# A 31-tap convolution between three engines: the low halves of 32 weight chunks made by accumulating DMAs, and twelve taps of each odd block moved from TensorE to VectorE

## The chip, the cores and the metric

The kernel runs on one core of one Trainium2 chip. The metric is the device time of one execution in microseconds (us). Before the change it is 2404.21 us, the median of 3 runs (2402.06 to 2404.46).

## The reference

Two layers over a residual stream of 256 tokens by 2048 channels, in float32. What matters here is the first layer's conformer group:

```
u = rms_norm(h) @ w_in                      # 2048 -> 4096, split into a_val, a_gate, xr, gr (1024 each)
ya = a_val * sigmoid(a_gate)                # GLU, 1024 channels
ya = causal_depthwise_conv(ya, conv_a_w, conv_a_b)     # 31 taps for each channel
ya = silu(layer_norm(ya, ln_a_g, ln_a_b))
yb = rg_lru(causal_depthwise_conv(xr, 4 taps)) * gelu(gr)
h  = h + concatenate([ya, yb]) @ w_out
```

After it come a squared-ReLU MLP (2048 -> 8192 -> 2048), a per-layer embedding with a sigmoid gate, and a second layer with stick-breaking attention and the same MLP and gate.

## The kernel before, in words

**Layout.** Activations are held transposed: a tile is 128 channels by 256 tokens. The weights stream from HBM in 812 chunks of 512 KB (128 partitions x 4 row tiles x 256 columns), numbered in one fixed order: `C_GLU` = 34 begins the GLU part of the input projection (32 chunks), `C_OUTB` = 66 the half of the output projection that takes the RG-LRU channels (16 chunks), `C_PLE0` = 82 the embedding projection.

**Splitting.** A product in float32 is made of three float32r products: hi x hi, hi x lo and lo x hi. So each chunk is split: ScalarE copies `raw` into the hi half of a slot of `spl`, rounding it (`split` of ScalarE, `copy` at L636), VectorE writes `raw - hi` into the lo half (`split` of VectorE, L1037), and TensorE uses both (`chunk`, L398 for the 512-column matmuls, L404 for the 256-column ones; 16 matmuls a chunk). `raw` has 4 buffers (`NRAW`) and `spl` has 8 slots (`NSPL`). The sync engine loads chunk m once the lo of chunk m - 4 is made (`lo_ready`); ScalarE writes slot m % 8 once TensorE has used chunk m - 8 (`chunk_used`). ScalarE and VectorE split chunk m + 8 in the place of their programs that belongs to chunk m.

**Groups.** 256 output channels are one group: 4 chunks in the GLU part, 2 in the output halves. A group has two PSUM banks in turn with the next one. At its end ScalarE copies the 256 columns of the cross products (`take_cross`), VectorE adds them to the rest (`take_sum`, L1073), and a group may only start when the sum of the group two before it is taken.

**The convolution.** The 8 blocks of 128 GLU channels are convolved in pairs. Pair c - 1 is convolved while the groups of pair c go through TensorE (`glu_pair(c)`, c = 1, 2, 3), and the last pair beside the first four groups of `C_OUTB`. The even block of a pair is wholly VectorE's (`conv`, L1363 to L1369): 31 taps that alternate between two partial sums. The odd block is shared: TensorE does `CA_PE` = 25 taps as products with diagonal matrices `dg` (L576), which ScalarE builds out of the identity (`tap_matrices`, L892), and VectorE does `CA_VE` = 6 (L1375, L1378). `conv_end` (L1388) adds the two. TensorE's taps stand in three portions in a pair: behind the first group (`taps(0)`), in the middle of the second (`taps(1)`) and behind it (`taps(2)`); in `C_OUTB` one quarter stands behind each of four groups.

**Order.** Every engine has its program written out, in order, with semaphores. In `glu_pair` VectorE does, for q = 0 to 7, four steps of `conv`, one tap of the odd block (q < 6), and one `split`; after q = 3 it takes the value group (`glu_value`), at the end the gate group (`glu_gate`), which waits for a sigmoid of ScalarE (L869). In the first pair two RG-LRU operations are added (L1399 and a `lo_of`). ScalarE does an eighth of the matrices and one split for each q, `take_cross` after q = 3 and 7, and then waits for VectorE before the sigmoid. After the four `C_OUTB` groups the LayerNorm follows: two reductions on VectorE, two small matmuls in the middle of groups 5 and 7, and a chain up to the embedding projection (L461). GpSimd issues no DMA and is idle after its first microseconds.

Of the kernel before, what the change touches and what calls it, by code (L numbers as in the profile page):

```python
# [30 lines left out]
T = 256  # L31
DA = D // 2
# [35 lines left out]

H_OUTB, H_OUTA, H_MLP0, H_GATE0, H_OUT1, H_MLP1, H_GATE1 = 0, 8, 16, 48, 56, 64, 96
NDG = 14  # L70
CA_PE = 25
CA_VE = CA - CA_PE
CSTEPS = CA + 1 + CA_VE
LAM_STEPS = 17


GAIN = 0
# [12 lines left out]
def trunk(nc, xT, pT, par, w_in, w_rg_a, w_rg_x, w_out, w_qkv, w_o, w_up, w_down, w_proj, w_gate, outT):  # L90
    with ExitStack() as ctx:
# [3 lines left out]
        def sem(name):  # L95
            return ctx.enter_context(nc.semaphore(name))
# [58 lines left out]
        raw_landed = [sem(f"raw_landed{i}") for i in range(NRAW)]  # L155
        hi_ready = sem("hi_ready")
        lo_ready = sem("lo_ready")
        chunk_used = sem("chunk_used")
        par_landed = sem("par_landed")
        x_landed = [sem(f"x_landed{i}") for i in range(4)]  # L160
# [69 lines left out]
        def counts(base, turns):  # L230


            return base > 0 or not isinstance(turns, int)

        def bcast(ap, n):
            return ap.unsqueeze(1).broadcast_to([P, n, ap.shape[-1]])

# [11 lines left out]
        def _(sp):  # L249
            def load(m, it, src):  # L250

                if counts(m - NRAW + 1, it):
                    sp.wait_ge(lo_ready, it * 8 + (m - NRAW + 1))
                sp.dma_start(raw[:, m % NRAW, :, :], src).then_inc(raw_landed[m % NRAW], 16)

            def load_group(m, it, w, col, row0=0, rows=(0, 4, 8, 12)):
                for j, r in enumerate(rows):
                    src = w[bass.ds(row0 + r * P, 4 * P), bass.ds(col, 256)]
                    load(m + j, it, src.rearrange("(t p) n -> p t n", p=P))
# [39 lines left out]

            def half_square(m, w, row0):  # L300

                with sp.Fori(0, 2) as i:
                    for s in range(4):
                        load_group(m + 2 * s, i, w, i * 1024 + 256 * s, row0, (0, 4))

            def load_x(k):
                sp.dma_start(h[:, 4 * k:4 * k + 4, :], xT[4 * k * P:(4 * k + 4) * P, :].rearrange(
# [22 lines left out]
            with sp.Fori(1, 4) as i:  # L330
                load_group(C_REC, i, w_in[0], i * 256 + 2 * DA)
                load_group(C_REC + 4, i, w_in[0], i * 256 + 2 * DA + DB)
            with sp.Fori(0, 4) as i:
                load_group(C_GLU, i, w_in[0], i * 256)
                load_group(C_GLU + 4, i, w_in[0], i * 256 + DA)
            half_square(C_OUTB, w_out[0], DA)
            load_ple(C_PLE0, 0)
            half_square(C_OUTA, w_out[0], 0)
# [42 lines left out]
                               pattern=[[1, P]], channel_multiplier=-1).then_inc(consts_ready, 1)  # L381


        @block.tensor
        def _(pe):
            def chunk(b, m, it, x, kt0, first, last, tokens_out=False, releases=1):

                pe.wait_ge(lo_ready, it * 8 + (m + 1))
                w = spl[:, m % NSPL, :, :, :]
                for q in range(4):  # L390
                    kt, start, stop = kt0 + q, first and q == 0, last and q == 3
                    for o in range(2):
                        c = slice(o * P, (o + 1) * P)
                        if tokens_out:

                            pe.matmul(ps[:, b + o, :], x[:, kt, 0, c], w[:, q, :, :], start=start, stop=False)  # L396
                        else:
                            pe.matmul(ps[:, b + o, :], w[:, q, 0, c], x[:, kt, :, :], start=start, stop=False)  # L398
                    for o in range(2):
                        c = slice(o * P, (o + 1) * P)  # L400
                        if tokens_out:
                            mm = pe.matmul(ps[:, b + o, 0:256], x[:, kt, 1, c], w[:, q, 0, :], start=False, stop=stop)  # L402
                        else:
                            mm = pe.matmul(ps[:, b + o, 0:256], w[:, q, 1, c], x[:, kt, 0, :], start=False, stop=stop)  # L404
                mm.then_inc(chunk_used, releases)
# [44 lines left out]
            def ple(g, m, layer, units):  # L450

                for u in units:
                    c, b = m + 1 + u // 2, 2 * (u % 2)
                    pe.wait_ge(sum_ready, g + u - 1)
                    pe.wait_ge(lo_ready, c + 1)
                    for k in range(2):
                        x = spl[:, m % NSPL, 2 * layer + k, :, :]
                        for o in range(2):

                            w = spl[:, c % NSPL, 2 * k + u % 2, :, o * P:(o + 1) * P]  # L460
                            pe.matmul(ps[:, b + o, :], w[:, 0, :], x, start=(k == 0), stop=False)  # L461
                            mm = pe.matmul(ps[:, b + o, 0:256], w[:, 1, :], x[:, 0, :], start=False, stop=(k == 1))
                    if u < 7:
                        mm.then_inc(ple_done, 1)
                    else:
                        mm.then_inc(chunk_used, 5)
# [113 lines left out]
            gemm(G_GLU, 0, C_GLU, 0, XA)  # L580
            pe.wait_ge(rg_act, 4)
            gemm(G_GLU + 1, 0, C_GLU + 4, 0, XA)
            with pe.Fori(1, 4) as c:
                for s in range(2):
                    def taps(part):
                        conv(c - 1, c * CA_PE - CA_PE, part, 3)

                    gemm(G_GLU + s, c * 2, C_GLU + 4 * s, c, XA, mid=None if s == 0 else lambda: taps(1))
                    taps(2 * s)


# [42 lines left out]
        def _(act):  # L634
            def copy(out, in_, scale=1.0):
                return act.activation(out, in_, ACT.Copy, scale=scale)  # L636

            def split(m, it=0):

                if m < CHUNKS:  # L640
                    act.wait_ge(raw_landed[m % NRAW], it * (16 * 8 // NRAW) + 16 * (m // NRAW + 1))
                    if counts(m - NSPL + 1, it):
                        act.wait_ge(chunk_used, it * 8 + (m - NSPL + 1))
                    copy(spl[:, m % NSPL, :, 0, :], raw[:, m % NRAW, :, :]).then_inc(hi_ready, 1)

            def period(m, it, k=4):
                for q in range(k):
# [247 lines left out]
            def glu_pair(c):  # L895
                for q in range(8):
                    tap_matrices(c - 1, c * CA_PE - CA_PE, q, 8)
                    split(C_GLU + NSPL + q, c)
                    if isinstance(c, int) and q == 4:

                        act.wait_ge(rg_vec, 6)
                        copy(XB[:, 8:16, 0, :], pp[:, 0:8, :]).then_inc(rg_act, 1)
                    if q % 4 == 3:
                        take_cross(G_GLU + q // 4, c * 2, group_done(C_GLU + q - 3, c))
                glu_gate(c)

            act.wait_ge(rg_vec, 5)
            glu_pair(1)
            with act.Fori(2, 4) as c:
                glu_pair(c)  # L910

            def ple_cross(g, m, layer, units):
# [118 lines left out]
        def _(dve):  # L1031
            def split(m, it=0):

                if m < CHUNKS:
                    dve.wait_ge(hi_ready, it * 8 + (m + 1))
                    s = spl[:, m % NSPL, :, :, :]
                    dve.tensor_tensor(s[:, :, 1, :], raw[:, m % NRAW, :, :], s[:, :, 0, :].bitcast(F32),  # L1037
                                      ALU.subtract).then_inc(lo_ready, 1)
# [304 lines left out]
            def conv(pair, base, q):  # L1343
# [3 lines left out]

                first, y2t, second = y[:, bass.ds(pair * 2, 1), :], y2[:, :].unsqueeze(1), y[:, bass.ds(pair * 2 + 1, 1), :]

                def step(n):  # L1350
                    return n + min(n // 4, CA_VE)

                if q == 0:
                    dve.wait_ge(glu_ready, pair + 1)
                for n in range(4 * q, 4 * q + 4):
# [12 lines left out]
                    else:  # L1368
                        r = dve.tensor_tensor(first, first, y2t, ALU.add)  # L1369
                    r.then_inc(conv_step, 1)  # L1370
                if q < CA_VE:
                    k = CA_PE + q
                    x, w = glu[:, bass.ds(pair * 2 + 1, 1), k:k + T], par_col(pair * (2 * CA) + (CONV_A_W + CA + k))
                    if q == 0:
                        r = dve.tensor_scalar(second, x, w, par_col(pair * 2 + (1 + CONV_A_B)), ALU.mult, ALU.add)  # L1375
                    else:
                        dve.wait_ge(conv_step, base + 5 * q)
                        r = dve.scalar_tensor_tensor(out=second, in0=x, scalar=w, in1=second, op0=ALU.mult, op1=ALU.add)  # L1378
                    r.then_inc(conv_step, 1)
                if q == 7:  # L1380
                    dve.wait_ge(conv_step, base + CSTEPS)

# [7 lines left out]
            def glu_pair(c):  # L1390
                for q in range(8):
                    conv(c - 1, c * CSTEPS - CSTEPS, q)
                    split(C_GLU + NSPL + q, c)
                    if q == 3:
                        glu_value(c)
                    if isinstance(c, int) and q == 2:

                        dve.wait_ge(rg_vec, 5)
                        dve.tensor_tensor(pp[:, 0:8, :], r_, pp[:, 8:16, :], ALU.mult).then_inc(rg_vec, 1)  # L1399
                    if isinstance(c, int) and q == 6:  # L1400
                        dve.wait_ge(rg_act, 8)
                        lo_of(XB, 8, 8, pp[:, 0:8, :]).then_inc(yb_tiles, 1)
                glu_gate(c, lambda: conv_end(c - 1))

            glu_pair(1)
            with dve.Fori(2, 4) as c:
                glu_pair(c)

            def ple_sums(g, units):
# [183 lines left out]
```

## Time and profile before

| what | value |
|---|---|
| median of 3 runs | 2404.21 us |
| profiled execution, its own time | 2405.38 us |
| its span | 2403.7 us |
| TensorE clock granted, mean | 0.992 |
| TensorE busy | 2353.1 us (98%) |
| VectorE busy | 1600.6 us (67%) |
| ScalarE busy | 1277.2 us (53%) |
| GpSimd busy | 2.1 us |

Shares are over the whole span; a stage has its own. A busy share of TensorE says that matmuls are in flight, not that they run at their peak. Idle time of an engine counts only if another waits for it. The convolution stands between about 155 and 279 us of the span.

### The profile page before, as it was taken

The numbers are of one execution on the slowest core, as the hardware profiler recorded it, in microseconds if no ns is written. First come the engines' busy times: TensorE is split into PE (matmuls) and PEld (weight loads), VectorE is DVE, ScalarE is ACT, GpSimd is POOL, SyncE is SP. The second block draws the span as 40 slices with busy tenths as digits, with TensorE's granted clock in tenths as the row PEclk, the third lists the DMA queues.
The fourth block names the chain that finished last, engine by engine and source line by source line (L and its number), as shares of the span: only waits on it lengthen the run. The fifth ranks groups of instructions, "written<-read, shape, count | busy, mean of one in ns | idle before, by whom it ended". The sixth has DMA issues, their size and how long they took to land.

```text
span 2403.7 us, 39317 instructions
## 1 busy us (share of the span) xinstructions
PE 2353.1 (98%) x13454; PEld 2052.8 (85%) x13454; DVE 1600.6 (67%) x1892; ACT 1277.2 (53%) x1632; POOL 2.1 (0%) x15
## 2 busy tenths in 40 slices
PE   7999999999999999999999999999999999999997
PEld 6878878888888888888888888888888888888886
DVE  7789987655555555667766666766556556556665
ACT  6665565444444545555565666555445445445553
POOL 0000000000000000000000000000000000000000
PEclk9999999999999999999999999999999999999998
DMA  7644456655665666555655554656656566565553
GB/s 232 210 123 135 130 163 193 193 185 182 197 187 181 195 189 185 187 189 166 201 172 177 168 157 142 208 183 189 193 180 198 185 187 192 188 188 187 190 161 105
DMA packets 432146, 431.03 MB, mean 179 GB/s; under 512 B 13136, under 2 KB 430032, under 8 KB 432080
## 3 DMA queue, kind: packets, MB, share of 16 engines
q1 hardware_dynamic: 432080, 430.20, 57.5%
q8 instruction: 36, 0.59, 0.1%
q14 instruction: 30, 0.25, 0.0%
HBM read 428.05 MB, written 2.10 MB: 179 GB/s over the span
## 4 chain that ended last, share of the span: by engine, by line
PE 91%; DVE 4%; ACT 2%; issue 1%; DMA 1%; DVEq 0%; SPq 0%; ACTq 0%
PE ps L398 56%; PE ps L404 28%; PE ps L396 2%; PE O L576 2%; DVE spl L1037 1%; PE ps L402 1%; ACT spl L636 1%; PE ps L461 0%; PE O L505 0%; DVE tv L1073 0%; PE Z L479 0%; DMA raw<-in_w_o 0%; DMA raw<-in_w_in 0%; DVE nacc L1101 0%; DVE tv L1099 0%
## 5 line engine op out<-in xcount | busy, mean ns | idle before, releaser
L1037 DVE TENSOR_TENSOR spl<-raw,spl 128x1024 fp32r<-128x1024 f32 x810 | 979.6, 1223 | 521.1 <-ACT spl L636 482.5
L636 ACT ACTIVATE spl<-raw 128x1024 fp32r<-128x1024 f32 x810 | 842.9, 1055 | 685.6 <-PE ps L404 640.9
L398 PE MATMUL ps<-XA,spl 128*128 128x512 f32 x3072 | 971.1, 398 | 15.9 <-DVE spl L1037 10.9
L398 PE MATMUL ps<-XB,spl 128*128 128x512 f32 x3072 | 967.5, 396 | 0.5 <-DVE pp L1073 0.5
L404 PEld LDWEIGHTS ps<-XA,spl 128*128 128x128 f32 x3072 | 579.2, 189 | 137.2
L404 PEld LDWEIGHTS ps<-XB,spl 128*128 128x128 f32 x3072 | 577.1, 188 | 136.4
L404 PE MATMUL ps<-XA,spl 128*128 128x256 f32 x3072 | 605.2, 278 | 0.0
L404 PE MATMUL ps<-XB,spl 128*128 128x256 f32 x3072 | 603.6, 278 | 0.0
L398 PEld LDWEIGHTS ps<-XA,spl 128*128 128x128 f32 x3072 | 470.4, 189 | 17.6 <-issue 11.5
L398 PEld LDWEIGHTS ps<-XB,spl 128*128 128x128 f32 x3072 | 468.3, 189 | 1.6 <-issue 0.8
L1073 DVE TENSOR_TENSOR tv<-cross,ps 128x512 f32<-128x512 f32 x208 | 141.6, 681 | 39.4 <-ACT cross L636 39.2
L636 ACT ACTIVATE cross<-ps 128x512 f32<-128x512 f32 x224 | 130.3, 582 | 68.8 <-PE ps L404 57.2
L716 ACT ACTIVATE tv<-tv 128x512 f32<-128x512 f32 x64 | 40.4, 631 | 138.5 <-DVE tv L1130 138.5
L1117 DVE TENSOR_TENSOR h<-h,tv 128x512 f32 (+1 forms) x104 | 72.0, 692 | 21.1 <-DVE tv L1073 18.8
L396 PE MATMUL ps<-spl,XB 128*128 128x512 f32 x256 | 80.7, 397 | 0.0
L689 ACT ACTIVATE tv<-h 128x512 f32 (+1 forms) x56 | 35.4, 632 | 59.0 <-DVE h L1117 56.1
L1066 DVE TENSOR_TENSOR XB<-tv,XB 128x512 f32 (+1 forms) x32 | 22.2, 692 | 54.0 <-ACT XB L636 54.0
L402 PEld LDWEIGHTS ps<-spl,XB 128*128 128x128 f32 x256 | 48.1, 188 | 11.4
L1066 DVE TENSOR_TENSOR XA<-tv,XA 128x512 f32 (+1 forms) x32 | 22.2, 692 | 53.4 <-ACT XA L636 53.4
L576 PE MATMUL O<-glu,dg 128*128 (+1 forms) x200 | 47.1, 389 | 3.7 <-ACT dg L892 3.7
L402 PE MATMUL ps<-spl,XB 128*128 128x256 f32 x256 | 50.4, 278 | 0.0
L1367 DVE SCALAR_TENSOR_TENSOR y<-glu,params,y 128x256 f32<-128x256 f32 (+1 forms) x116 | 48.7, 478 | 0.8 <-DVE glu L1079 0.5
(145 smaller groups left out, 885.7 us busy)
## 6 DMA issues: line engine op xcount, KB each, us to landing
raw<-in_w_up SPq DMA_DIRECT2D x256, 512.0 KB, 3.9
raw<-in_w_down SPq DMA_DIRECT2D x256, 512.0 KB, 3.5
raw<-in_w_qkv SPq DMA_DIRECT2D x96, 512.0 KB, 4.4
raw<-in_w_in SPq DMA_DIRECT2D x64, 512.0 KB, 4.2
raw<-in_w_gate SPq DMA_DIRECT2D x64, 512.0 KB, 4.3
raw<-in_w_out SPq DMA_DIRECT2D x32, 512.0 KB, 3.4
raw<-in_w_o SPq DMA_DIRECT2D x32, 512.0 KB, 4.6
raw<-in_w_proj SPq DMA_DIRECT2D x8, 512.0 KB, 4.3
```

Source lines behind the costliest of these rows:

```text
L396: pe.matmul(ps[:, b + o, :], x[:, kt, 0, c], w[:, q, :, :], start=start, stop=False)
L398: pe.matmul(ps[:, b + o, :], w[:, q, 0, c], x[:, kt, :, :], start=start, stop=False)
L402: mm = pe.matmul(ps[:, b + o, 0:256], x[:, kt, 1, c], w[:, q, 0, :], start=False, stop=stop)
L404: mm = pe.matmul(ps[:, b + o, 0:256], w[:, q, 1, c], x[:, kt, 0, :], start=False, stop=stop)
L576: pe.matmul(O[:, 0, 0:256], dg[:, k % NDG, :], glu[:, bass.ds(pair * 2 + 1, 1), k:k + T], start=(k == 0), stop=(k == CA_PE - 1), skip_grou ...
L636: return act.activation(out, in_, ACT.Copy, scale=scale)
L716: act.activation(tv[:, :, :], tv[:, :, :], ACT.Square).then_inc(up_sq, 1)
L1037: dve.tensor_tensor(s[:, :, 1, :], raw[:, m % NRAW, :, :], s[:, :, 0, :].bitcast(F32), ALU.subtract).then_inc(lo_ready, 1)
L1066: return dve.tensor_tensor(X[:, bass.ds(t0, n), 1, :], v, X[:, bass.ds(t0, n), 0, :].bitcast(F32), ALU.subtract)
L1073: dve.tensor_tensor(tv[:, :, :] if out is None else out, cross[:, :, :], ps[:, b:b + 2, 0:256], ALU.add).then_inc(sum_ready, 1)
L1117: dve.tensor_tensor(ht, ht, tv[:, :, :], ALU.add).then_inc(res_ready, 1)
L1367: r = dve.scalar_tensor_tensor(out=o, in0=x, scalar=w, in1=o, op0=ALU.mult, op1=ALU.add)
```

## The change

The 32 chunks 50 to 81 (`SUMMED`) get their lo in another way. ScalarE writes hi as before and then also -hi, a second copy with scale -1, into the lo half. GpSimd waits for it and issues an accumulating DMA from `raw` onto the lo half, SBUF to SBUF, so that raw - hi stands there. TensorE and the load that reuses the `raw` buffer wait for that DMA. VectorE has no split for them. `CA_PE` goes from 25 to 13, so VectorE does 18 taps of each odd block, spread evenly over the 32 steps of `conv`. Some loops (`Fori`) of the sync, tensor, scalar and vector programs are written out, as the chunk number must be known.

```
-CA_PE = 25
+CA_PE = 13
+SUMMED = tuple(range(C_GLU + 16, C_PLE0))
+def cuts(m):
+    return m - sum(1 for k in SUMMED if k < m)
+def sums(m):
+    return sum(1 for k in SUMMED if k < m and k % NSPL == m % NSPL)
...
+        def lo_there(engine, m, it):
+            if m in SUMMED:
+                engine.wait_ge(lo_summed[m % NSPL], 16 * sums(m) + 16)
+            elif counts(m + 1, it):
+                engine.wait_ge(lo_ready, it * 8 + cuts(m + 1))
...                                             # sync, load()
-                if counts(m - NRAW + 1, it):
-                    sp.wait_ge(lo_ready, it * 8 + (m - NRAW + 1))
+                lo_there(sp, m - NRAW, it)
...                                             # gpsimd
+            for n, m in enumerate(SUMMED):
+                pool.wait_ge(neg_ready, n + 1)
+                pool.dma_start(spl[:, m % NSPL, :, 1, :].bitcast(F32), raw[:, m % NRAW, :, :],
+                               accum_op=ALU.add).then_inc(lo_summed[m % NSPL], 16)
...                                             # tensor, chunk() and ple()
-                pe.wait_ge(lo_ready, it * 8 + (m + 1))
+                lo_there(pe, m, it)
...                                             # scalar, split()
+                    if m in SUMMED:
+                        copy(spl[:, m % NSPL, :, 1, :], raw[:, m % NRAW, :, :], -1.0).then_inc(neg_ready, 1)
...                                             # vector, split()
-                if m < CHUNKS:
+                if m < CHUNKS and m not in SUMMED:
...                                             # vector, conv()
+                def seconds(n):
+                    return n * CA_VE // (CA + 1)
                 def step(n):
-                    return n + min(n // 4, CA_VE)
+                    return n + seconds(n)
...
-                if q < CA_VE:
-                    k = CA_PE + q
...
+                    if seconds(n + 1) > seconds(n):
+                        j = seconds(n)
+                        x = glu[:, bass.ds(pair * 2 + 1, 1), CA_PE + j:CA_PE + j + T]
...
+                            dve.wait_ge(conv_step, base + n0 + 1 + j)
+                            r = dve.scalar_tensor_tensor(out=second, in0=x, scalar=w, in1=second,
+                                                         op0=ALU.mult, op1=ALU.add)
```

## Rows read from the trace of the kernel before

**Rows 1.** The page: span; busy us, share, instructions by engine.
```profile
span 2403.7 us, 39317 instructions
PE 2353.1 (98%) x13454; PEld 2052.8 (85%) x13454; DVE 1600.6 (67%) x1892; ACT 1277.2 (53%) x1632; POOL 2.1 (0%) x15
```

**Rows 2.** Windows: stretch, length; PE, PEld, DVE, ACT, POOL busy; clock, DMA, GB/s.
```profile
154.90:279.00 124.10, 124.10 (x654) 108.03 (x655) 117.38 (x212) 69.52 (x143) 0.00 (x0) 0.99 0.43 133
301.50:325.00 23.50, 18.60 (x86) 14.95 (x85) 17.52 (x20) 18.54 (x27) 0.00 (x0) 0.85 0.23 69
```

**Rows 3.** The chain of waits in order of time: start, us, what.
```profile
154.87 5.40 PE O L576 x16
189.95 3.46 PE O L576 x16
199.00 3.46 PE O L576 x16
208.05 3.89 PE O L576 x18
241.18 3.89 PE O L576 x18
275.17 3.02 PE O L576 x14
```

**Rows 4.** Who waited for whom from 154.9 to 279 us: total, times, longest.
```profile
ACT spl L636 <- PE ps L404: 32.5, 20, 4.3
ACT tv L869 <- DVE tv L1079: 18.0, 3, 9.5
PE O L576 <- ACT dg L892: 3.7, 1, 3.7
```

**Rows 5.** Timeline of VectorE, second pair: start, us, instruction, tiles, idle before.
```profile
190.84 1.67 DVE L1367 SCALAR_TENSOR_TENSOR y<-glu,params,y  x4
192.42 0.48 DVE L1378 SCALAR_TENSOR_TENSOR y<-glu,params,y  x1
192.82 1.22 DVE L1037 TENSOR_TENSOR spl<-raw,spl 128x1024 fp32r<-128x1024 f32 x1
193.95 1.67 DVE L1367 SCALAR_TENSOR_TENSOR y<-glu,params,y  x4
200.19 0.68 DVE L1073 TENSOR_TENSOR tv<-cross,ps 128x512 f32<-128x512 f32 x1
201.99 1.90 DVE L1367 SCALAR_TENSOR_TENSOR y<-glu,params,y  x4 [0.27 <-DVE glu L1079]
214.17 0.68 DVE L1073 TENSOR_TENSOR tv<-cross,ps 128x512 f32<-128x512 f32 x1
217.91 0.41 DVE L1363 TENSOR_SCALAR y<-glu,params  x1 [0.93 <-DVE glu L1312]
```

**Rows 6.** Groups by line: the RG-LRU product of the first pair, on VectorE.
```profile
L1399 DVE TENSOR_TENSOR pp<-rg,pp 128x2048 f32<-128x2048 f32 x1 | 2.3, 2283 | 0.0
```

**Rows 7.** Tile y, each pair's last step: ns min/median/max, first to last start.
```profile
L1388 DVE TENSOR_TENSOR y<-y,O x4: 410/414/420, 185.9 to 279.1; 128x256 f32<-128x256 f32 x2, 128x256 f32 x2
```

**Rows 8.** Timeline of ScalarE: the start, and two rows of the second pair.
```profile
153.76 0.97 ACT L892 ACTIVATE dg<-ident,params 128x128 f32<-128x128 f32 x3
189.27 1.04 ACT L636 ACTIVATE spl<-raw 128x1024 fp32r<-128x1024 f32 x1
190.22 0.97 ACT L892 ACTIVATE dg<-ident,params 128x128 f32<-128x128 f32 x3
```

**Rows 9.** DMA: page's queue; issues in two stretches; a window of the sync engine.
```profile
q1 hardware_dynamic: 432080, 430.20, 57.5%
raw<-in_w_in SPq DMA_DIRECT2D x12, 512.0 KB, 3.7
h<-in_xT SPq DMA_DIRECT2D x4, 512.0 KB, 8.7
10.00:20.00 10.00, 1.00 1.10 352
```

More of the change, by code:

```diff
@@ L157, in trunk @@
         lo_ready = sem("lo_ready")
+        neg_ready = sem("neg_ready")
+        lo_summed = [sem(f"lo_summed{i}") for i in range(NSPL)]
         chunk_used = sem("chunk_used")
@@ L300, in half_square @@
             def half_square(m, w, row0):
-                with sp.Fori(0, 2) as i:
-                    for s in range(4):
-                        load_group(m + 2 * s, i, w, i * 1024 + 256 * s, row0, (0, 4))
+                for s in range(8):
+                    load_group(m + 2 * s, 0, w, 256 * s, row0, (0, 4))
             def load_x(k):
@@ L332, in _ @@
                 load_group(C_REC + 4, i, w_in[0], i * 256 + 2 * DA + DB)
-            with sp.Fori(0, 4) as i:
-                load_group(C_GLU, i, w_in[0], i * 256)
-                load_group(C_GLU + 4, i, w_in[0], i * 256 + DA)
+            for i in range(4):
+                load_group(C_GLU + 8 * i, 0, w_in[0], i * 256)
+                load_group(C_GLU + 8 * i + 4, 0, w_in[0], i * 256 + DA)
             half_square(C_OUTB, w_out[0], DA)
@@ L454, in ple @@
                     pe.wait_ge(sum_ready, g + u - 1)
-                    pe.wait_ge(lo_ready, c + 1)
+                    lo_there(pe, c, 0)
                     for k in range(2):
@@ L582, in _ @@
             gemm(G_GLU + 1, 0, C_GLU + 4, 0, XA)
-            with pe.Fori(1, 4) as c:
+            for c in range(1, 4):
                 for s in range(2):
@@ L586, in taps @@
                         conv(c - 1, c * CA_PE - CA_PE, part, 3)
-                    gemm(G_GLU + s, c * 2, C_GLU + 4 * s, c, XA, mid=None if s == 0 else lambda: taps(1))
+                    gemm(G_GLU + 2 * c + s, 0, C_GLU + 8 * c + 4 * s, 0, XA, mid=None if s == 0 else lambda: taps(1))
                     taps(2 * s)
@@ L897, in glu_pair @@
                     tap_matrices(c - 1, c * CA_PE - CA_PE, q, 8)
-                    split(C_GLU + NSPL + q, c)
-                    if isinstance(c, int) and q == 4:
+                    split(C_GLU + NSPL + 8 * c + q)
+                    if c == 1 and q == 4:
                         act.wait_ge(rg_vec, 6)
@@ L903, in glu_pair @@
                     if q % 4 == 3:
-                        take_cross(G_GLU + q // 4, c * 2, group_done(C_GLU + q - 3, c))
+                        take_cross(G_GLU + 2 * c + q // 4, 0, group_done(C_GLU + 8 * c + q - 3, 0))
                 glu_gate(c)
@@ L908, in _ @@
             glu_pair(1)
-            with act.Fori(2, 4) as c:
+            for c in range(2, 4):
                 glu_pair(c)
@@ L1370, in conv @@
                     r.then_inc(conv_step, 1)
-                if q < CA_VE:
-                    k = CA_PE + q
[L1373 to L1379, printed above, removed]
+                    if seconds(n + 1) > seconds(n):
+                        j = seconds(n)
+                        x = glu[:, bass.ds(pair * 2 + 1, 1), CA_PE + j:CA_PE + j + T]
+                        w = par_col(pair * (2 * CA) + (CONV_A_W + CA + CA_PE + j))
+                        if j == 0:
+                            r = dve.tensor_scalar(second, x, w, par_col(pair * 2 + (1 + CONV_A_B)), ALU.mult, ALU.add)
+                        else:
+                            n0 = max(k for k in range(n) if seconds(k + 1) > seconds(k))
+                            dve.wait_ge(conv_step, base + n0 + 1 + j)
+                            r = dve.scalar_tensor_tensor(out=second, in0=x, scalar=w, in1=second,
+                                                         op0=ALU.mult, op1=ALU.add)
+                        r.then_inc(conv_step, 1)
                 if q == 7:
@@ L1392, in glu_pair @@
                     conv(c - 1, c * CSTEPS - CSTEPS, q)
-                    split(C_GLU + NSPL + q, c)
+                    split(C_GLU + NSPL + 8 * c + q)
                     if q == 3:
                         glu_value(c)
-                    if isinstance(c, int) and q == 2:
+                    if c == 1 and q == 2:
                         dve.wait_ge(rg_vec, 5)
                         dve.tensor_tensor(pp[:, 0:8, :], r_, pp[:, 8:16, :], ALU.mult).then_inc(rg_vec, 1)
-                    if isinstance(c, int) and q == 6:
+                    if c == 1 and q == 6:
                         dve.wait_ge(rg_act, 8)
@@ L1405, in _ @@
             glu_pair(1)
-            with dve.Fori(2, 4) as c:
+            for c in range(2, 4):
                 glu_pair(c)
```

## The prediction

> **What bounds the kernel now.** I read the page first: TensorE is busy for 98% of the span [rows 1], so only what shortens TensorE's path, or makes it wait, can count. The windows come next. From 154.9 to 279 us, where the convolution runs, TensorE is busy all 124.1 us, VectorE 117.4 and ScalarE 69.5; the DMA engines are at 0.43 and GpSimd does nothing [rows 2]. The chain of waits says what TensorE does there: chunks, and between them portions of taps, which lie on the chain themselves [rows 3]. The waits show that it hardly waits (3.7 us for the first matrices), while ScalarE waits 32.5 us for TensorE's slots and 18.0 us for VectorE's end of a pair [rows 4]. So TensorE bounds this stage, with VectorE close behind, and room is on ScalarE, GpSimd and the DMA engines.
>
> **Unit prices.** On TensorE a tap is two records, so nine take 3.89 us: 0.432 a tap. The portion in the middle of a group ends at 199.00 + 3.46 = 202.46, and the next begins at 208.05, with two chunks between: 5.59 us, 2.79 a chunk [rows 3]. On VectorE four taps and the next start are 192.42 - 190.84 = 1.58 us, 0.395 a tap; a lo difference takes 193.95 - 192.82 = 1.13 of its queue. glu_value takes 201.99 - 200.19 = 1.80 and glu_gate with its waits 217.91 - 214.17 = 3.74 [rows 5]. On ScalarE a rounding copy takes 190.22 - 189.27 = 0.95 and a matrix 0.97 / 3 = 0.32 [rows 8].
>
> **TensorE's taps.** 4 x 12 = 48 taps go, 48 x 0.432 = 20.7 us, all on the path. I walk through it. Portions are now 4, 4 and 5 taps. The first one still waits for ScalarE: from 153.76 [rows 8] it builds a matrix, then copy and negated copy, two matrices, again two copies, and the fourth matrix at 153.8 + 4 x 0.32 + 4 x 0.95 = 158.9 us; the portion ends at about 159.4 instead of 154.87 + 5.40 = 160.3 [rows 3]. Then two chunks, 4 taps, two chunks, 5 taps: 174.5. Four chunks on, the second pair's taps start at 185.7, where they started at 189.95. A pair is then 8 x 2.79 + 13 x 0.432 = 27.9 us, against 33.1 (208.05 to the like portion at 241.18). So the third pair's taps start at 213.6, the output groups at 230.4 (241.18 + 3.89 = 245.1 before), and the last tap ends at 230.4 + 27.9 = 258.3 against 275.17 + 3.02 = 278.2 [rows 3]. If nobody is late, 19.9 us are gained.
>
> **VectorE.** A pair is 49 taps x 0.395 = 19.4, 0.4 for the sum of the two partials, 1.8 and 3.7: 25.3 us; eight differences (9.0 us) left it and twelve taps (4.7) came. The first pair has two more operations of 2.3 us [rows 6] (the second taken as equal): 29.9. It begins about with TensorE's first portion, at 154.7, and the GLU values are ready at 184.6, where TensorE asks at 185.7; then at 209.9, asked at 213.6; the third time at about 235.2, asked at 230.4 + 5.6 = 236.0. The cover is thin, 0.8 us in places. The last pair, 19.8 us and four times 1.4 for the output sums, ends at 261.0, 2.7 us behind TensorE, where its last step began at 279.1 [rows 7] behind 278.2. The chain of the LayerNorm hangs on it and TensorE waits in it later (18.6 of 23.5 us busy [rows 2]). I charge 1.4 us, between 0 (the small matmuls stand further back in groups 5 and 7) and 4 (each tap 0.02 us dearer by its wait).
>
> **ScalarE.** 32 negated copies at 0.95 are 30.4 us more, 48 matrices at 0.32 are 15.4 less. A pair: 16 x 0.95 + 13 x 0.32 + about 2 of crosses and sigmoid (estimated as two copies) = 21 of 27.9 us. Its waits of 32.5 us [rows 4] cover it: nothing. Each cross stands 0.95 later, with a whole group of cover. If the cover were gone it would be at most 12 x 0.95 = 11 us.
>
> **The loops written out** change loads' order in nothing; 0, at most 1 us either way (no row prices a loop's turn).
>
> **The accumulating DMAs.** No row shows one, nor a DMA issued by GpSimd. What they must do follows from the walk. TensorE wants chunk 50's lo at 174.5 and chunk 81's at 258.3 + 7 x 2.79 = 277.8. ScalarE has the first negated copy done at 153.8 + 0.3 + 1.9 = 156.0. Landing: 3.7 us is the nearest load, 8.7 the longest one, those of x behind each other [rows 9]; I take 5, so the first lo is there at 161. Then 31 more may take 277.8 - 161 = 116.8 us, 3.77 us each, before TensorE loses anything. Two limits decide whether that holds.
> - Engine time. A load occupies the 16 engines for 57.5% x 2403.7 / 821 = 1.68 us on average, 524 KB / 352 GB/s = 1.49 when they are full [rows 9]. Beside each load stands now one accumulate of X us. Below it is a plain copy, 1.49. It reads two operands and writes one, three passes where a copy has two: 2.24. With both reads in one line, it is two loads' worth: 2.98 at the full rate, 3.36 at the average. At 2.24 the pace is 3.73, just under 3.77: no stall.
> - Latency. A raw buffer is held for load, two copies and accumulate: (3.7 + 1.9 + 0.3 + L) / 4. L = 5 gives 2.7 us a chunk, 8.7 gives 3.65: no stall. From L = 9.2 it stalls.
> I take X at 2.24, as the queue's 1.49 and 1.68 hold waiting on HBM that a read of SBUF need not have.
>
> The Trainium skill speaks against it in "Collectives: The Full Stack", The bandwidth ceiling: a reduce step has two read descriptors for each chunk on the same read ring, so it runs at about half a copy's rate. That is the second rival's X; no run here shows it so far. Its page "DMA: Bandwidth & Descriptors", Anatomy of one DMA, gives a GpSimd-issued DMA 2.0 us plus bytes / 436 GB/s, by which L would be an estimated 3.2 us and the latency limit harmless.
>
> **Sum.** 2405.4 (the profiled execution) - 19.9 + 1.4 = 2386.9. The profile lies 1.2 us above the median, so 2385.7: I say 2386.
>
> **The rivals.**
> 1. *The DMA engines become the bound, two reads for one.* X = 2.98: pace 4.47, stall 31 x (4.47 - 3.77) = 21.7, net 21.7 - 18.5 = +3.2: 2407. X = 3.36 beside loads of 1.68: pace 5.04, stall 39.4: 2425. TensorE would wait for lo from the third pair on. It decides from X = 2.88, where the pace is 3.77 + 18.5 / 31 = 4.37. For it: 8 chunks of the output part come at 2.79 us with no tap between. Against: a share of only 0.43 now.
> 2. *The slot is held too long.* GpSimd's issuing and the landing take L = 12 us or more, and as all accumulates stand in one queue behind one another, a chunk takes 4.5 us or more: 2407 at 4.5, 2422 at 5, 2453 at 6. From L = 11.6 it is slower than before. For it: GpSimd is a slow issuer for all the rows tell (none), and 8.7 us exists in this trace as a landing. Against: loads land in 3.7 us.
> 3. *Half a stall.* X between 2.3 and 2.9: 2388 to 2404.
> 4. *VectorE is the bound*, each tap at its own 0.48 us [rows 5] instead of 0.395: a pair is 29.5 us, 1.6 above TensorE's, over four pairs some 6 us: 2392. It is part of the forecast's case.
>
> **How the numbers follow.** About 0.2% (4.8 us) is what a measurement of this kernel can tell from no change. Forecast with rival 4: 0.50, all faster, its own range 2381 to 2394. Rival 3: 0.10, of it 0.04 faster, 0.06 within. Rival 1: 0.22, of it 0.08 within and 0.14 slower. Rival 2: 0.18, slower. Faster 0.54, same 0.14, slower 0.32. The range goes from 2381 (no charge for VectorE, taps a little dearer than 0.432) to 2430, which takes in rival 1 and the nearer half of rival 2.
>
> **What would show it.** Right: TensorE still busy throughout from 155 to 258, 104 tap records, the last tap at about 258, VectorE without a difference there, a pair of 27.9 us, ScalarE waiting for slots. The accumulate's landing, the DMA share of the stretch (0.43 now; over 0.9 for rival 1, below it with a long landing for rival 2) and TensorE's waits for a DMA onto the lo half tell the rivals apart. The forecast is wrong if such waits exceed 3 us in total, or if ScalarE's waits turn from TensorE's slots to loads.

## The result, and the profile after

The changed kernel takes 2417.18 us (median of 6 runs, 2411.0 to 2419.44) against 2403.62 of before (6 runs, 2402.06 to 2405.34): ratio 1.0053, 95% interval 1.0042 to 1.0063. It is slower by 13.6 us; 18 us faster was forecast.

The page of the changed kernel, its first rows:

```profile
span 2417.7 us, 38500 instructions
PE 2343.0 (97%) x13358; PEld 2038.5 (84%) x13358; DVE 1582.7 (65%) x1908; ACT 1292.7 (53%) x1616; POOL 43.2 (2%) x47
```

TensorE is busy 10 us less than in [rows 1] and the span is 14 us longer, so it waits. (The taps that left are worth 20.7 us; the rest of its work took longer at the lower granted clock of this stage, 0.89 against 0.99.) The tile y says where: VectorE's addition of TensorE's partial sum (before: [rows 7], last at 279.1) and the first reduction of the LayerNorm.

```profile
L1424 DVE TENSOR_TENSOR y<-y,O x4: 414/415/420, 183.3 to 294.5; 128x256 f32<-128x256 f32 x4
L1464 DVE TENSOR_REDUCE nacc<-y x1: 3866/3866/3866, 295.0 to 295.0; 128x256 f32<-128x2048 f32 x1
```

The same reduction before:

```profile
L1428 DVE TENSOR_REDUCE nacc<-y x1: 3872/3872/3872, 279.5 to 279.5; 128x256 f32<-128x2048 f32 x1
```

The LayerNorm begins 15 us later than before and the span ends 14 us later: the whole loss arises in the convolution. The window of that stage (length; PE, PEld, DVE, ACT, POOL busy; clock; DMA share; GB/s), which answers to [rows 2]:

```profile
155.00:292.00 137.00, 115.43 (x555) 96.10 (x556) 95.72 (x220) 83.93 (x126) 39.68 (x31) 0.89 1.11 223
```

No compute engine is full any more. The DMA share went from 0.43 to 1.11 (packets in flight together are counted each, so it can pass 1; loads alone, at their fullest, gave 1.10 in [rows 9]). The DMA view of the same stretch (packets, MB, share of the 16 engines; issues: count, size, median us to landing), which answers to [rows 9]:

```profile
q0 software_dynamic: 15834, 15.73, 78.1%
q1 hardware_dynamic: 14821, 14.72, 33.1%
spl<-raw POOLq DMA_DIRECT2D x31, 512.0 KB, 8.5
raw<-in_w_out SPq DMA_DIRECT2D x16, 512.0 KB, 6.3
raw<-in_w_in SPq DMA_DIRECT2D x12, 512.0 KB, 7.3
```

An accumulate is one of the accumulating DMAs. One of 512 KB is 528 packets, so the 15834 packets are 30 of them, and they took 0.781 x 137 us of the 16 engines: 3.57 us each. This packet time of one transfer is called its engine time below. A load's is 0.331 x 137 / 28 = 1.62. Landing is the time from a DMA's issue to its end. GpSimd's timeline, the first and the last of its 32 issues:

```profile
154.88 1.44 POOL L406 DMA_DIRECT2D spl<-raw  x1 [152.14 <-ACT spl L662]
157.35 1.29 POOL L406 DMA_DIRECT2D spl<-raw  x1 [1.03 <-ACT spl L662]
292.13 1.30 POOL L406 DMA_DIRECT2D spl<-raw  x1 [1.10 <-ACT spl L662]
```

(292.13 - 154.88) / 31 = 4.43 us a chunk. The waits from 150 to 293 us, which answer to [rows 4]:

```profile
DVE tv L1101 <- ACT cross L662: 39.3, 8, 9.6
ACT spl L662 <- DMA raw<-in_w_in: 25.2, 8, 7.0
ACT spl L662 <- DMA raw<-in_w_out: 23.0, 12, 6.4
PE O L602 <- ACT dg L920: 22.1, 12, 6.7
PE O L602 <- DVE glu L1340: 3.6, 1, 3.6
```

ScalarE no longer waits for TensorE's slots but 48 us for loads; TensorE waits for ScalarE's matrices. It never waits for a lo half. The chain of waits shows the loop (start, us, what):

```profile
178.54 9.87 DMA spl<-raw
188.43 8.03 DMA raw<-in_w_in
199.07 1.90 ACT spl L662 x2
201.25 10.11 DMA spl<-raw
211.38 8.43 DMA raw<-in_w_in
```

An accumulate must land before a load reuses its raw buffer, and that load before ScalarE may split. From the accumulate at 178.54 to the one at 201.25, which is five chunks on, it is 22.7 us: 4.5 a chunk.

### The profile page after: what moved, and what is told of

Same layout as the page of the kernel before. It is cut to its first block, busy times and chain, and to the rows that moved or that the text cites. A ratio compares the mean times of both kernels' runs of the same rounds, so it can differ in the third digit from the quotient of the medians.

```text
span 2417.7 us, 38500 instructions
## 1 busy us (share of the span) xinstructions
PE 2343.0 (97%) x13358; PEld 2038.5 (84%) x13358; DVE 1582.7 (65%) x1908; ACT 1292.7 (53%) x1616; POOL 43.2 (2%) x47
## 4 chain that ended last, share of the span: by engine, by line
PE 85%; DMA 6%; DVE 5%; ACT 3%; issue 2%; DVEq 0%; POOL 0%; SPq 0%; ACTq 0%; POOLq 0%
PE ps L424 53%; PE ps L430 26%; DMA spl<-raw 3%; PE ps L422 2%; DVE spl L1065 1%; DMA raw<-in_w_in 1%; ACT spl L662 1%; DMA raw<-in_w_out 1%; PE ps L428 1%; DVE tv L1101 0%; PE O L531 0%; PE Z L505 0%; DMA raw<-in_w_o 0%; DVE nacc L1129 0%; PE ps L487 0%
## 5 line engine op out<-in xcount | busy, mean ns | idle before, releaser
L1065 DVE TENSOR_TENSOR spl<-raw,spl 128x1024 fp32r<-128x1024 f32 x778 | 940.4, 1224 | 520.5 <-ACT spl L662 483.5
L662 ACT ACTIVATE spl<-raw 128x1024 fp32r<-128x1024 f32 x842 | 873.1, 1054 | 699.5 <-PE ps L430 596.9
L1145 DVE TENSOR_TENSOR h<-h,tv 128x512 f32 (+1 forms) x104 | 72.0, 692 | 19.9 <-DVE tv L1101 17.6
L602 PE MATMUL O<-glu,dg 128*128 128x256 f32 x104 | 34.8, 473 | 25.6 <-ACT dg L920 22.1
L1399 DVE SCALAR_TENSOR_TENSOR y<-glu,params,y 128x256 f32<-128x256 f32 x116 | 51.5, 480 | 0.2
```

Source lines behind the costliest of these rows:

```text
L1145: dve.tensor_tensor(ht, ht, tv[:, :, :], ALU.add).then_inc(res_ready, 1)
L1399: r = dve.scalar_tensor_tensor(out=o, in0=x, scalar=w, in1=o, op0=ALU.mult, op1=ALU.add)
```

## The experiments

Three theories. **A:** the 16 DMA engines are full, because an accumulate holds them for 3.6 us. **B:** the ring of four raw buffers is too slow by its latency (load, two copies, GpSimd, landing), whatever the engines' load. **C:** part of the loss is ScalarE's order, in which matrices and crosses (the copies of the cross products) stand behind a split whose load is late. Times are medians; the ratio is to the kernel before on the same chip.

**1. Copy instead of add**

```
-                               accum_op=ALU.add).then_inc(lo_summed[m % NSPL], 16)
+                               ).then_inc(lo_summed[m % NSPL], 16)
```

> The 32 GpSimd DMAs copy raw onto the lo half instead of adding it (the sum is left out, so the lo half holds the whole weight; same bytes written, half the bytes read). Theory A, engine time: an accumulate fills the 16 DMA engines for about 3 us because it reads two operands; as a copy it takes 1.5 to 1.7, load and copy together 3.2 us a chunk, under the 3.77 that the convolution leaves, so about 2387 us and a DMA share near 0.9 or less. Theory B, latency: a raw buffer is held for load, two copies and a GpSimd DMA with a long fixed part; the copy then lands in 6 us or more and the time stays above 2400 us.

2388.03 us, ratio 0.9929 (0.9912 to 0.9945). Its DMA view from 155 to 292 us:

```profile
q0 software_dynamic: 4608, 16.78, 36.2%
spl<-raw POOLq DMA_DIRECT2D x31, 512.0 KB, 5.2
```

0.362 x 137 / 32 = 1.55 us of engine time instead of 3.57. As A expected. All else of the change is in this kernel, the negated copies, GpSimd's waits and the moved taps, so none of that makes the loss. The copy also has fewer packets and lands 3.3 us earlier, so this run alone does not exclude B.

**2. Half the bytes, both operands**

```
-                pool.dma_start(spl[:, m % NSPL, :, 1, :].bitcast(F32), raw[:, m % NRAW, :, :],
+                pool.dma_start(spl[:, m % NSPL, 0:2, 1, :].bitcast(F32), raw[:, m % NRAW, 0:2, :],
```

> All 32 accumulating DMAs stay, with their waits, but each adds only two of the four row tiles (the other two keep -hi, so half of the lo is left wrong). Theory A (engine time, 3.5 us an accumulate, by the byte): 1.8 us an accumulate and 3.4 with the load, under the budget of 3.77: 2386 to 2390 us, with both operands still read. Theory B (a fixed time through GpSimd and back in the raw ring): the landing hardly falls, 2400 us or more.

2386.96 us, 0.9923 (0.9908 to 0.9938). Its DMA view:

```profile
q0 software_dynamic: 8704, 8.39, 41.3%
spl<-raw POOLq DMA_DIRECT2D x32, 256.0 KB, 5.7
```

And its taps in the tile dg (duration min/median/max, first and last start):

```profile
L602 PE MATMUL O<-glu,dg x104: 377/378/792, 154.0 to 259.0; 128*128 128x256 f32 x104
```

0.413 x 137 / 32 = 1.77 us, half of 3.57 for half the bytes and about half the packets (272). GpSimd issues as often and nearly as long (1.20 us against 1.28), so its work is not the bound. But the landing fell as well, from 8.5 to 5.7 us, against what B had expected: this run doesn't tell A from B either. GpSimd's first and last issue:

```profile
155.74 1.34 POOL L406 DMA_DIRECT2D spl<-raw  x1 [152.99 <-ACT spl L662]
261.25 1.21 POOL L406 DMA_DIRECT2D spl<-raw  x1 [1.03 <-ACT spl L662]
```

That is 3.40 us a chunk, and 3.39 in 1, where the full kernel has 4.43.

**3. The addend from HBM, the raw buffer free earlier**

```
-                pool.dma_start(spl[:, m % NSPL, :, 1, :].bitcast(F32), raw[:, m % NRAW, :, :],
+                # src: the same 512 KB of w_in or w_out
+                pool.dma_start(spl[:, m % NSPL, :, 1, :], src.rearrange("(t p) n -> p t n", p=P).bitcast(F32R),
...                                             # sync, load()
+                if m - NRAW in SUMMED:
+                    sp.wait_ge(neg_ready, SUMMED.index(m - NRAW) + 1)
```

> The accumulating DMA takes its addend from the weights in HBM and not from raw, and the next load waits only for the negated copy, so the raw buffer is free some 8.5 us earlier while the DMA engines do the same work. Theory A (the 16 engines are full, 4.4 us a chunk): nothing gained, 2412 us or more, DMA share about 1. Theory B (the raw ring, (6.5 + 2 + 8.5 + waits) / 4 = 4.4 us a chunk): the ring takes under 3 us a chunk, about 2387 us.

2409.81 us, 1.0022 (1.0013 to 1.0032). Its DMA view:

```profile
q0 software_dynamic: 15712, 15.62, 70.7%
spl<-in_w_in POOLq DMA_DIRECT2D x16, 512.0 KB, 18.4
```

And its window:

```profile
155.00:292.00 137.00, 120.40 (x613) 101.47 (x614) 105.99 (x231) 88.69 (x132) 41.18 (x32) 0.94 1.15 237
```

Just under A's range and far above B's: 7 us came back, so the ring (B) has a part, but most of the loss stayed. With the ring open the transfers queue at the engines (landing 18.4 us, share 1.15): A.

**4. Larger pieces**

```
-        spl = sb("spl", [P, NSPL, 4, 2, 256], F32R)
+        spl = sb("spl", [P, NSPL, 2, 4, 256], F32R)[:, :, :, :, :].rearrange("p s h t n -> p s t h n")
```

> The slots of spl are laid out as [hi/lo][row tile][column], so the accumulating DMA writes 4 KB in one piece per partition instead of four of 1 KB; bytes, waits and everything else are the same. Theory A with a cost by descriptor: engine time of an accumulate falls from about 3 us towards 2.2, pace under 3.8, 2387 to 2395 us. Theory A with a cost by byte: the same 3 us and 2417 us. Theory B: the landing falls by under 1 us, 2410 us or more.

2412.62 us, 1.0029 (1.0017 to 1.004). Engine time 0.671 x 137 / 32 = 2.87 us, landing 7.6, share 1.02. An accumulate is now 144 packets (4607 for 32), as the copy of 1 is, so the two compare: 2.87 against 1.55 is what the adding costs, with its second read (no run parts the read from the addition), and 3.57 against 2.87 is the smaller pieces. The engine time fell, but not to the 2.2 that A needed for its 2387 to 2395 us; with a load of 1.55 it is still 4.4 us a chunk. B's expectation, the landing under 1 us shorter and 2410 us or more, is what came.

**5. Matrices first (C)**

```
-                    tap_matrices(c - 1, c * CA_PE - CA_PE, q, 8)
+                    if q == 0:
+                        tap_matrices(c - 1, c * CA_PE - CA_PE, 0, 1)
...                                             # and the like ahead of the C_OUTB groups
```

> ScalarE builds all 13 matrices of a pair at once, ahead of the pair's first split, instead of one or two before each split. Theory C: the stall is passed on in ScalarE's order, where matrices and cross copies stand behind a split that waits for its load 8 chunks ahead; the waits for matrices (22 us of matmul) go, cross copies stay late, 2405 to 2412 us. If only the pace of the lo counts, nothing changes: 2417 us.

2425.28 us, 1.0093 (1.0076 to 1.011). Its waits from 150 to 293 us:

```profile
DVE tv L1102 <- ACT cross L662: 36.2, 8, 7.3
PE O L602 <- DVE glu L1341: 28.3, 4, 11.7
```

Slower than either expectation. The waits for matrices are gone and 28.3 us of waits for the GLU values stand in their place. A likely reason for the 8 us more, argued and not tested: four us of matrices (13 x 0.32) ahead of each pair's splits are four us in the loop of the raw buffers.

**6. Crosses first (C)**

```
+                    if q % 4 == 3:
+                        take_cross(G_GLU + 2 * c + q // 4, 0, group_done(C_GLU + 8 * c + q - 3, 0))
                     split(C_GLU + NSPL + 8 * c + q)
...
-                    if q % 4 == 3:
-                        take_cross(G_GLU + 2 * c + q // 4, 0, group_done(C_GLU + 8 * c + q - 3, 0))
...                                             # and the like in the four C_OUTB groups
```

> The changed kernel with ScalarE's cross copies put ahead of the split that stands before them and waits for the same chunk of TensorE. Theory C (part of the loss is that work TensorE waits for stands behind a split whose load is late): VectorE's 39 us of waits for crosses shrink, TensorE is freed earlier, 2410 to 2414 us. If the pace of the DMA engines sets the end whatever ScalarE's order is: 2417 us.

2417.27 us, 1.0056 (1.0039 to 1.0073): nothing, though VectorE's waits for crosses shrank from 39.3 to 32.1 us. C as it was put falls: neither order brings anything back. ScalarE's order is not without weight, as 5 lost 8 us by it.

**7. The taps alone**

```
-SUMMED = tuple(range(C_GLU + 16, C_PLE0))
+SUMMED = ()
```

> The moved taps alone: no chunk is summed by a DMA, VectorE makes all differences and has 18 taps of each odd block. A pair is then 25.3 + 8 x 1.13 = 34.3 us on VectorE (38.9 in the first) against TensorE's 27.9; from 154.7 us the last step would come at 38.9 + 2 x 34.3 + 34.8 = 142.3, 297 us, against 279: about 2421 us, bound by VectorE.

2417.27 us, 1.0052 (1.0035 to 1.0069), 4 us under the walk: VectorE was busy for 134.82 of 137 us, and TensorE waited 20.3 us for its GLU values. The moved taps pay only if the differences leave VectorE.

**8. The accumulates alone**

```
-CA_PE = 13
+CA_PE = 25
```

> The accumulating DMAs alone: all 32 lo halves by DMA, but TensorE keeps its 25 taps. Theory A: the DMA engines need 31 x 4.43 us from 155 us whatever the taps are, while TensorE needs the last tap at 278 and chunk 81 at 297: the pace allowed is 4.35, so only a small stall, 2405 to 2415 us. ScalarE has 48 matrices more, 15 us, in the loop that fills the raw buffers: if that loop is what counts, up to 2430 us.

2415.17 us, 1.0046 (1.0029 to 1.0063), just above A's range. The same time as the whole change within the runs' spread: 20.7 us of taps more on TensorE cost nothing, as it was not the bound. The 48 matrices more on ScalarE did not bring the 2430 us either.

**9. Every second chunk**

```
-SUMMED = tuple(range(C_GLU + 16, C_PLE0))
+SUMMED = tuple(range(C_GLU + 16, C_PLE0, 2))
-CA_PE = 13
+CA_PE = 19
```

> Only every second chunk of the 32 gets its lo by an accumulating DMA (16 of them), and TensorE keeps 19 taps, so that VectorE, which has 16 differences back, stays under it. Theory A (engine time 3.5 us an accumulate, 1.6 a load): two chunks cost 6.7 us, 3.4 a chunk, under the budget of 3.77; the whole gain of 24 taps x 0.432 = 10.4 us shows, 2394 to 2397 us. If something else than the DMA load of an accumulate holds the kernel up (the wait through GpSimd, the negated copies), half of the 31 us of delay stays: about 2408 us.

2403.01 us, 0.9994 (0.9985 to 1.0004): a miss for A, and 5 us under the other expectation. The share of the stage is 0.84, two chunks cost 3.54 + 2 x 1.7 = 6.9 us of engine time, 3.5 a chunk, and still the 10.4 us of the taps don't show. Its waits:

```profile
ACT spl L662 <- PE ps L430: 26.6, 18, 4.2
ACT spl L662 <- DMA raw<-in_w_out: 12.3, 4, 6.0
PE O L602 <- ACT dg L920: 7.1, 3, 5.7
```

**10. The same with the addend from HBM** (the edits of 3 and 9)

> Every second chunk summed and 19 taps on TensorE, as before, and the addend comes from HBM, so the raw buffer is free after the two copies. The like kernel with its addend from raw gained nothing at a DMA share of 0.84. Theory B for what was left there (every second raw buffer is held for load, copies and landing, about 15.5 us for four chunks): the 10.4 us of the taps now show, 2393 to 2397 us. Theory A: the engines have no less to do, 2403 us.

2393.43 us, 0.9954 (0.994 to 0.9968). Its window:

```profile
155.00:292.00 137.00, 136.12 (x729) 118.22 (x728) 128.98 (x234) 87.21 (x146) 20.66 (x16) 0.98 0.85 203
```

Its DMA view:

```profile
q0 software_dynamic: 8448, 8.39, 41.0%
spl<-in_w_in POOLq DMA_DIRECT2D x8, 512.0 KB, 8.3
```

And its waits:

```profile
ACT spl L670 <- PE ps L438: 38.1, 25, 3.7
```

As B expected of the rest: the DMA share is that of 9 (0.85 against 0.84), the landing no shorter (8.3 against 6.9), only the buffer is free earlier, and 9.6 us come. ScalarE waits for TensorE again and for no load. This version beats both kernels.

**11. Every second chunk, larger pieces** (the edits of 4 and 9)

> Every second chunk summed, 19 taps, and spl laid out so that an accumulate writes 4 KB pieces (2.9 us of engine time instead of 3.5 in the full kernel, landing 0.9 us earlier). Theory B for the rest: the ring is 0.9 us shorter for four chunks, 2399 to 2402 us. Theory A: the share falls from 0.84 to 0.77, 2399 to 2403 us. It does not tell the two apart; it shows whether the layout pays.

2401.82 us, 0.9985 (0.9976 to 0.9995), 1 to 2 us under 9 and inside both ranges. Share 0.76, engine time 0.321 x 137 / 16 = 2.75 us, landing 6.7 against 6.9. A fifth less engine time for each accumulate brought next to nothing here.

**12. All that helped** (the edits of 3, 4, 6 and 9)

> The version that the runs point to: every second chunk summed, addend from HBM, 4 KB destination pieces, the cross copies ahead of the split, 19 taps on TensorE. Engine time no bound (share under 0.85), ring short, cross copies early: 2392 to 2396 us, faster than both kernels. If a landing of over 10 us from HBM comes too late for TensorE's slot: above 2400 us.

2393.96 us, 0.9954 (0.994 to 0.9967), as 10. The layout brings nothing when the source rows are 1 KB (engine time 0.411 x 137 / 16 = 3.52 us). More raw buffers, the direct test of B, were not tried.

## Why the prediction was wrong

**Held.** TensorE's walk: the last tap was put at 258.3 us; in 2, where the DMAs keep up, the last tap record starts at 259.0, and in 1 at 257.4. VectorE's 49 taps run at 0.395 us (rows of 0.88 us for two, next start 0.79 later), and the 2386 us are what 1 and 2 measure, 2388 and 2387. So the terms of -19.9 and +1.4 were right in their sum; in their parts less so, as VectorE's last step, put to end at 261.0, starts at 263.8 in 2.

**The step that failed** is "I take X at 2.24". It was reasoned that an accumulate makes three passes where a copy has two, and that a read of SBUF would not hold the waiting on HBM. Measured are 3.57 us, 2.3 times the copy's 1.55 between the same buffers (1.85 times in packets of the copy's size, by 4), above even the 2.98 to 3.36 of the first rival. 3.57 + 1.62 = 5.19 us of engine time a chunk, run at 4.43 as packet times overlap, does not fit in 3.77.

The rule of the Trainium skill that was set aside (Collectives: The Full Stack, The bandwidth ceiling: two read descriptors, about half a copy's rate) comes near: 1.85 times a copy's engine time with packets of the same size, but 2.3 times in this kernel, with its smaller ones.

**The budget** of 3.77 us was wrong too, which 1 and 2 hide. It counts up to TensorE's use of chunk 81 at 277.8. But ScalarE splits 8 chunks ahead, and matrices and crosses stand behind a split in its program, so a late load is felt long before its chunk is used. Where nothing is lost, in 1 and 2, GpSimd issues every 3.4 us. The time beyond 2387 us goes with the pace above that: 31 x (pace - 3.40) gives 2410 for 3 (pace 4.13), 2412 for 4 (4.19), 2417 for 6 (4.38), 2419 for the full kernel (4.43) and 2423 for 5 (4.56), within 2.3 us of their medians. This is a gauge and not a cause: it says that the whole loss is the delay of these issues, and 3.4 fits as the pace that they had to keep. That the 8 chunks ahead are the reason is argued from the programs; what the trace shows is TensorE's 22.1 us of waits for matrices and none for a lo half. With 3.77 the full kernel would have come to 2406. And by the sums of engine time 9 and 11, at 3.5 a chunk and less, should have lost nothing.

**The landing** was taken as 5 us and is 8.5; at that latency the ring stalls nothing by the formula of the prediction, (3.7 + 1.9 + 0.3 + 8.5) / 4 = 3.6. But the load in it was left at 3.7, and beside accumulates it takes 6.3 to 7.3: 4.3 to 4.5 us a chunk. The Trainium skill (DMA: Bandwidth & Descriptors, Anatomy of one DMA) would put the landing at an estimated 3.2 us; even the copies of 1 need 5.2 here. So both limits of the prediction were passed together, and each was priced as if the other had room. 3 takes the ring's limit away and gets 7 us back; halving the engine time (2) gets all of it back, by shortening the ring too. With 16 accumulates the engines have room and the ring alone costs 9.6 us (9 against 10).

**The rivals.** The first comes nearest: an accumulate costs at least two loads, the share is over the 0.9 that it named, and 2417 lies in its 2407 to 2425 us; its chance was 0.22. (The skill's rule is that rival's, not the second's as the prediction has it.) That the number fits is in part luck: by its formula the measured 3.57 us give a pace of 5.19 and 2430 us, and two errors offset each other, as the true pace was lower (4.43) and the pace allowed was lower too (3.4). It said that TensorE would wait for lo halves; it waited for matrices and GLU values, by ScalarE's order as above. A sign that the forecast is wrong was named rightly: ScalarE's waits turned from TensorE's slots to loads, 48 us.

The second rival, the slot held too long, has a part: its landing of 12 us did not come (8.5), but slower loads made the ring as slow. Its GpSimd is no bound: it issues in 1.28 us and waits for ScalarE before each issue.

**What stays open** is, in the full kernel, how much of the 4.43 us is queueing at full engines and how much the ring's own latency. Both fall together in 1 and 2; 3 puts what freeing the buffer alone gives back at 7 us of the 30 between 2417 and 2387.

## What to carry to other kernels

An operation moved to idle DMA engines is not free: price it in engine time for each chunk, with two reads for an accumulate, and compare the sum with load and accumulate against the chunk's period; then price the latency loop of the buffer it holds, with the loads as slow as they are beside it. If the loop is what binds, feed the accumulate from a source that does not hold the scarce buffer. Here it took both: half of the work with the addend from HBM gained 10 us, half of it alone nothing (9), all of it with the addend from HBM lost some 5 (3), and all of it as it was lost 14.

## What the runs showed of the hardware

- An accumulating DMA of 512 KB, SBUF to SBUF in 1 KB pieces, takes 3.57 us of the 16 DMA engines' time, a copy between the same places 1.55 (in 144 packets, where the accumulate has 528); half the bytes take 1.77; with 4 KB pieces at the destination, 144 packets, 2.87.
- With the addend from HBM the figure is about the same (3.25 in 3, 3.51 in 10), so reading it from SBUF saves nothing.
- Beside the accumulates a load of 512 KB lands in 6.3 to 7.3 us, where it landed in 3.4 to 3.7 in the same stage before, though its own engine time did not grow (1.62; the prediction's 1.68 over the whole span).
- GpSimd is occupied 1.28 us by issuing such a DMA, 0.86 us with 4 KB pieces and 0.75 us for the plain copy.
- TensorE's granted clock was 0.89 in the stage with its waits, 0.99 before and 0.98 in 10, where it hardly waits.
